# First up stage: the spread steps dealt 1, 2, 1, 2, 2 to the tiles, and a tile's first operands built ahead of the multiplication of kept results

## Chip, cores and metric

The kernel runs on 1 core of one Trainium2 chip. The metric is the device time of one execution in microseconds, median over several runs; lower is better.

## What is computed

A model of two blocks in float32, 256 tokens of width 2048 (with 16 meta tokens ahead in the first block): an HGRN2 layer, a forgetting attention layer, a layer of convolution and sliding-window attention, and at the end the PEER layer, the only part that matters here:

```python
def peer(xn, peer_w_q, peer_sub_keys, peer_u, peer_v):
    ...
    qh = (xt @ peer_w_q).reshape(T, PEER_HEADS, 2, PEER_HALF)
    sub = jnp.einsum("thpc,hpnc->thpn", qh, peer_sub_keys).astype(jnp.float32)
    ...
    experts = e1 * N_KEYS + e2
    gates = jax.nn.softmax(vals, axis=-1).astype(xn.dtype)
    def chunk_fn(args):
        xc, ec, gc = args
        u_sel = jnp.take(peer_u, ec, axis=0)
        h = jnp.einsum("cd,chkd->chk", xc, u_sel)
        a = jax.nn.gelu(h, approximate=False) * gc
        v_sel = jnp.take(peer_v, ec, axis=0)
        return jnp.einsum("chk,chkd->cd", a, v_sel)
```

Each token chooses 8 x 16 = 128 of 16,384 experts (128 x 128 keys).

## The kernel before

The kernel doesn't gather experts. It computes the product of all tokens with all experts and multiplies it by a dense table of coefficients, zero where an expert was not chosen. The experts are 128 **tiles** of 128, taken in two segments of 64. In each segment an **up stage** multiplies the tokens with tiles of `peer_u`, and a **down stage** multiplies the coefficients with tiles of `peer_v`.

Weights are float32, and each tile is split in two parts so that the product keeps its precision. For each half of a tile (1024 columns) ACT writes the high part `whi` (`split_hi`, L429), and then the low part `wlo = raw - whi` is formed (`split_lo`, L436), in this stage on DVE (`both_lo`). TensorE (PE) multiplies in `up_project` (L2060 to L2062, 48 matmuls of 256 columns a tile). DVE takes the result out of PSUM with a row factor (`hidden`, L2196), ACT applies the Gelu (L2109), and DVE multiplies that by the coefficient later (`gated`, L2201).

The table of coefficients is built by 32 **spread steps** for a segment, 8 tokens each (`STEP = 8`), and these are dealt to the tiles of the up stage by `steps_of`. A step q is, in this order:

- **operands** on DVE (`operands`): one-hot keys `e_one` (L2158), one-hot rows `e_row` (L2160) and three products `e_col` (L2164), into one of two buffers, q % 2. It waits until PE has done step q-2.
- **the step** on PE (`spread_step`, L2049): 24 small matmuls into bank 3 or 4, placed behind the tile's `up_project`. It waits for the operands, and for ACT to have emptied the same bank of step q-2.
- in the first segment alone, **the multiplication of kept results** on DVE (`multiply_kept`, L2103): 32 of the segment's 64 tiles had their product computed during the routing stage and lie in `e_coef` already; they are multiplied by the new coefficients. It waits for the step on PE, and increments `multiplied`.
- **the copy** on ACT (`spread_in_of`, L2093) of the other 32 tiles' coefficients. In the first segment it waits for `multiplied`.

Each engine runs its instructions in the order in which they are written. A round j of the loops in `up_vector`, `up_scalar` and `up_tensor` belongs to tile j; the first segment's steps begin with tile 3 and end with tile 22 (`UP_FIRST = (3, 0)`). In round j DVE also makes the low parts of tile j+1, and ACT its high parts; the multiplications for the steps of tile j stand in DVE's round j+1, the copies for them at the end of ACT's round j, so ahead of the high parts of tile j+2.

Of the kernel before, what the change touches and what calls it, by code (L numbers as in the profile page):

```python
# [153 lines left out]
def need(eng, sem, value):  # L154

    if not static(value) or value > 0:
        eng.wait_ge(sem, value)
# [57 lines left out]
def build(nc, hT_in, params_in, consts_in, masks_in, pos_in, keys_in, w_in, u_in, v_in, out):  # L215
    with ExitStack() as ctx:
# [1760 lines left out]
        STEPS = SEQ // STEP  # L1977
# [26 lines left out]
        def up_ps(q):  # L2004
            return bank[U_BANKS[q % 4]][:, 0:SEQ]
# [3 lines left out]
        def steps_of(g_, j):  # L2009

            k = j - UP_FIRST[g_]
            upto = lambda k: min((8 * k + 4) // 5, STEPS)
            return range(upto(k), upto(k + 1)) if k >= 0 else ()

        def up_plan(g_):

            last = max(j for j in range(STATIC_UP) if steps_of(g_, j))
            end = STATIC_UP if N_UP[g_] == STATIC_UP else STATIC_UP - 1
            plan, hid, act, gated = [], 0, 0, 0
            for j in range(end + 1):  # L2020
                gates = range(gated, min(gated + 5, act) if last < j < end else act if j == end else gated)
                gated = gates.stop
                hids, acts = [], []
                while act < hid and (act < N_ACT or act - N_ACT < gated):
                    acts.append(act)
                    act += 1
                while j >= UP_FIRST[g_] and hid < j and (hid < N_ACT + 2 or hid - N_ACT - 2 < gated) and hid - 2 < act:
                    hids.append(hid)
                    hid += 1
                    while act < hid and (act < N_ACT or act - N_ACT < gated):  # L2030
                        acts.append(act)
                        act += 1
                rest = range(gated, j if j == end else gated)
                gated = rest.stop
                plan.append((gates, hids, acts, rest))
            assert hid == act == gated == end
            return plan
# [59 lines left out]
        def multiply_kept(ve, q):  # L2097

            ve.wait_ge(spread, q + 1)
            if q == 0:  # L2100
                ve.wait_ge(kept, EARLY)
            now = e.coef[:, 0:EARLY, q * STEP:(q + 1) * STEP]
            ve.tensor_tensor(now, S_BANKS[q % 2][:].rearrange("p (c e) -> p e c", c=STEP)[:, 0:EARLY, :], now,  # L2103
                             ALU.mult).then_inc(multiplied, 1)
# [10 lines left out]
        def first_lo(ve, g_):  # L2115
            ve.wait_ge(coef_hi_done, g_ * SEG + 1)
            ve.tensor_tensor(e.coef_lo[:, 0, :], e.coef[:, 0, :], e.coef_first[:].bitcast(F32), ALU.subtract)\
                .then_inc(coef_split, 1)
# [34 lines left out]
        def operands(ve, g_, q):  # L2153

            b, at = q % 2, q + g_ * STEPS
            now = slice(q * STEP, (q + 1) * STEP)
            need(ve, spread, at - 1)
            ve.tensor_tensor(pairs(e.one[:, b, :, :]), keys(g_ * SEG, SEG), per_token(e.slots[:, 1, now, :], SEG),  # L2158
                             ALU.is_equal).then_inc(one_set, 1)
            ve.tensor_tensor(pairs(e.row[:, b, :, :]), keys(0, SUBKEYS), per_token(e.slots[:, 0, now, :], SUBKEYS),  # L2160
                             ALU.is_equal)
            ve.wait_ge(one_set, at + 1)
            for w in range(3):
                last = ve.tensor_tensor(pairs(e.col[:, b, w, :, :]), pairs(e.one[:, b, :, :]),  # L2164
                                        per_token(e.gates[:, w, now, :], SEG), ALU.mult)
            last.then_inc(cols_set, 1)

        def pairs(ap):
            return ap.rearrange("p t (n b) -> p t n b", b=2)

        def keys(at, n):
            return e.iota[:, at:at + n].rearrange("p (t n b) -> p t n b", t=1, b=2).broadcast_to([P, STEP, n // 2, 2])

        def per_token(ap, n):
            return ap.rearrange("p t (n b) -> p t n b", n=1).broadcast_to([P, STEP, n // 2, 2])

        def gate_parts(ve, ch):
            ve.wait_ge(slots_in, 1)
            def twice(ap):
                return ap.rearrange("p (a b) -> p a b", b=1).broadcast_to([P, SEQ, 2])  # L2180

            ch.link(ve.tensor_copy(e.gates[:, 0, :, :], twice(e.slot_gate)))
            ch.link(ve.tensor_tensor(e.rest[:, 0, :], e.slot_gate, e.gates[:, 0, :, 0], ALU.subtract))
            ch.link(ve.tensor_copy(e.gates[:, 1, :, :], twice(e.rest[:, 0, :])))
            ch.link(ve.tensor_tensor(e.rest[:, 1, :], e.rest[:, 0, :], e.gates[:, 1, :, 0], ALU.subtract))
            ch.link(ve.tensor_copy(e.gates[:, 2, :, :], twice(e.rest[:, 1, :])))

        def both_lo(ve, t):
            for half in range(2):
                split_lo(ve, t, half)  # L2190
# [7 lines left out]
        def gated(ve, g_, j):  # L2198
            ve.wait_ge(gelu_done, j + 1 + UP_BEFORE[g_])
            k = UP_AT[g_] + j  # L2200
            ve.tensor_tensor(at3(e.coef, k), one3(e.act[:, j % N_ACT, :]), at3(e.coef, k), ALU.mult)\  # L2201
                .then_inc(coef_done, 1)

        def up_vector(ve, ch, g_):
            if g_ == 0:
                gate_parts(ve, ch)
                ve.wait_ge(w_lo_done[1], T_U[0] + UP_FIRST[0] + 1 - NATIVE)
            else:
                for q in steps_of(g_, 0):
                    operands(ve, g_, q)  # L2210
                flush(ve, g_ - 1)
            last = max(j for j in range(STATIC_UP) if steps_of(g_, j))
            for j, (gates, hids, _, rest) in enumerate(up_plan(g_)):
                steps = steps_of(g_, j)
                if g_ == 0:
                    for q in steps_of(g_, j - 1):
                        multiply_kept(ve, q)
                if j or g_ == 0:
                    for q in steps[:1]:
                        operands(ve, g_, q)  # L2220
                if j < STATIC_UP and (g_ or j >= UP_FIRST[0]):
                    both_lo(ve, Tile(T_U[g_], j // 4, j % 4).next())
                if j == last + 1:
                    ve.wait_ge(spread_in, STEPS * (g_ + 1))
                for k in gates:
                    gated(ve, g_, k)
                if j == N_UP[g_]:
                    first_lo(ve, g_)
                for k in hids:
                    hidden(ve, g_, k)  # L2230
                if j or g_ == 0:
                    for q in steps[1:]:
                        operands(ve, g_, q)
                for k in rest:
                    gated(ve, g_, k)
            if N_UP[g_] == STATIC_UP:
                return

            def body(i):
                for s in range(4):  # L2240
                    j, t = 4 * i + s, Tile(T_U[g_], i, s)
                    ve.wait_ge(halves_done, 2 * t.n)
                    need(ve, gelu_done, j - 2 + UP_BEFORE[g_])
                    ve.tensor_tensor(e.hid[:, (s + 1) % 2, :], up_ps(t.q + 3), rinv[:, 0:SEQ],
                                     ALU.mult).then_inc(evacuated, 1)
                    if within(j, N_UP[g_]):
                        both_lo(ve, t.next())
                    ve.wait_ge(gelu_done, j + UP_BEFORE[g_])
                    k = UP_AT[g_] + j - 1
                    ve.tensor_tensor(at3(e.coef, k), one3(e.act[:, 2 + (s + 1) % 2, :]), at3(e.coef, k),  # L2250
                                     ALU.mult).then_inc(coef_done, 1)
                    if static(j) and j == N_UP[g_]:
                        break
            with ve.Fori(STATIC_UP // 4, N_UP[g_] // 4) as i:
                body(i)
            first_lo(ve, g_)
            body(N_UP[g_] // 4)
# [77 lines left out]
        def flush(ve, g_):  # L2335
            ve.wait_ge(halves_done, 2 * (T_V[g_] + SEG))
            for b in FLUSHED_AT:
                h2 = hT[:, 2 * b:2 * b + 2, cols_q]
                need(ve, flushed, 8 * g_)
                ve.tensor_tensor(h2, bank[b][:].rearrange("p (a b) -> p a b", a=2), h2, ALU.add).then_inc(flushed, 1)  # L2340
# [205 lines left out]
```

## Time and profile before

| | us |
|---|---|
| median of 3 runs | 3059.23 (3058.94 to 3059.59) |
| the profiled execution, its own time | 3061.99 |
| its span, first to last instruction | 3060.2 |
| PE busy | 3002.7 (98%) |
| DVE busy | 1951.2 (64%) |
| ACT busy | 1637.0 (53%) |
| mean granted clock of TensorE | 0.994 |

The first up stage's spread steps lie between 1757.8 and 1903.2 us of the span. Busy shares tell how long an engine executes; with matmuls overlapping, PE counts as busy from the start of one to the modelled end of the last. An idle time is given in square brackets ahead of the instruction that waited, with what released it. Instructions on DVE and ACT are pipelined too: one's record may end some 0.08 us after the next one's start.

### The profile page before, as it was taken

What the parts mean: (1) busy time and instruction counts of PE and PEld (TensorE: products, weight loads), DVE (VectorE), ACT (ScalarE), POOL (GpSimd) and SP (SyncE); (2) the same over time, 40 slices, a digit from 0 to 9 for tenths busy, and PEclk for the clock granted to TensorE, in tenths of its full rate; (3) what the DMA queues carried; (4) which work ended last, traced back from release to release, by engine and by line L of the source; (5) the groups of instructions that cost most, each with busy time, mean ns of one, the idle gap of its engine ahead of it and who ended that gap; (6) DMA issues with size and microseconds to landing.
All of it is one profiled execution on the core that took longest, in us unless ns stands there. A gap on an engine that the chain in (4) does not pass through costs nothing.

```text
span 3060.2 us, 63442 instructions
## 1 busy us (share of the span) xinstructions
PE 3002.7 (98%) x25220; PEld 2945.3 (96%) x25220; DVE 1951.2 (64%) x3277; ACT 1637.0 (53%) x2636; POOL 662.6 (22%) x293
## 2 busy tenths in 40 slices
PE   8999998999999999989999999999999999999999
PEld 8999998999999998769999999999999999999999
DVE  6777776744544568757777788655458865554454
ACT  5777775566788643565444434444444444444443
POOL 3333333444444432114444300000000000000000
PEclk9999999999999999989999999999999999999999
DMA  5444443554434454325555534555554455555554
GB/s 197 148 149 150 151 151 124 171 174 166 166 138 149 147 177 152 118 77 190 178 181 178 180 137 150 182 191 184 187 192 162 157 180 187 183 192 184 187 191 165
DMA packets 72288, 506.67 MB, mean 166 GB/s; under 512 B 7904, under 2 KB 10464, under 8 KB 11232
## 3 DMA queue, kind: packets, MB, share of 16 engines
q1 hardware_dynamic: 71584, 503.16, 48.3%
q8 instruction: 91, 1.49, 0.2%
q10 hardware_dynamic: 576, 1.72, 0.2%
q14 instruction: 37, 0.30, 0.0%
HBM read 502.75 MB, written 2.10 MB: 165 GB/s over the span
## 4 chain that ended last, share of the span: by engine, by line
PE 93%; DVE 5%; ACT 2%; issue 1%; DMA 0%; SPq 0%; DVEq 0%; ACTq 0%
PE bank L453 12%; PE bank L452 12%; PE bank L454 12%; PE bank L466 5%; PE bank L2284 4%; PE banks L2284 4%; PE bank L2285 4%; PE banks L2285 4%; PE bank L2286 4%; PE banks L2286 4%; PE banks L2060 3%; PE banks L2061 3%; PE banks L2062 3%; PE bank L2060 3%; PE bank L2061 3%; PE bank L2062 2%
## 5 line engine op out<-in xcount | busy, mean ns | idle before, releaser
L429 ACT ACTIVATE whi<-raw 128x1024 fp32r<-128x1024 f32 x898 | 939.2, 1057 | 946.1 <-PE bank L454 367.9
L436 DVE TENSOR_TENSOR wlo<-raw,whi 128x1024 fp32r<-128x1024 f32 x667 | 851.3, 1288 | 445.9 <-ACT whi L429 445.0
L436 POOL TENSOR_TENSOR wlo<-raw,whi 128x1024 fp32r<-128x1024 f32 x231 | 605.6, 2622 | 947.7 <-ACT whi L429 947.6
L452 PE MATMUL bank<-xa_hi,whi 128*128 128x272 f32 (+1 forms) x2000 | 581.5, 291 | 6.8 <-DVE wlo L436 5.5
L453 PE MATMUL bank<-xa_lo,whi 128*128 128x272 f32 (+1 forms) x2000 | 572.8, 286 | 0.0
L454 PE MATMUL bank<-xa_hi,wlo 128*128 128x272 f32 (+1 forms) x2000 | 571.8, 286 | 0.0
L452 PEld LDWEIGHTS bank<-xa_hi,whi 128*128 128x128 f32 x2000 | 376.6, 188 | 10.4 <-issue 7.1
L453 PEld LDWEIGHTS bank<-xa_lo,whi 128*128 128x128 f32 x2000 | 377.9, 189 | 1.3
L454 PEld LDWEIGHTS bank<-xa_hi,wlo 128*128 128x128 f32 x2000 | 376.6, 188 | 0.0
L452 PE MATMUL bank<-xb_hi,whi 128*128 128x256 f32 (+1 forms) x1120 | 317.9, 284 | 1.5 <-DVE wlo L436 1.5
L453 PE MATMUL bank<-xb_lo,whi 128*128 128x256 f32 (+1 forms) x1120 | 316.3, 282 | 0.0
L454 PE MATMUL bank<-xb_hi,wlo 128*128 128x256 f32 (+1 forms) x1120 | 315.5, 282 | 0.0
L2285 PE MATMUL bank<-e_coef_lo,whi 128*128 128x256 f32 x1024 | 286.0, 279 | 0.0
L2285 PE MATMUL banks<-e_coef_lo,whi 128*128 128x256 f32 x1024 | 285.9, 279 | 0.0
L2284 PE MATMUL bank<-e_coef_hi,whi 128*128 128x256 f32 x1008 | 282.6, 280 | 0.0
L2284 PE MATMUL banks<-e_coef_hi,whi 128*128 128x256 f32 x1008 | 282.6, 280 | 0.0
L2286 PE MATMUL bank<-e_coef_hi,wlo 128*128 128x256 f32 x1008 | 278.8, 277 | 0.0
L2286 PE MATMUL banks<-e_coef_hi,wlo 128*128 128x256 f32 x1008 | 278.7, 277 | 0.0
L2060 PE MATMUL banks<-xb_hi,whi 128*128 128x256 f32 x768 | 216.2, 282 | 1.9 <-DVE hT L2340 1.3
L2061 PE MATMUL banks<-xb_lo,whi 128*128 128x256 f32 x768 | 215.9, 281 | 0.0
L2062 PE MATMUL banks<-xb_hi,wlo 128*128 128x256 f32 x768 | 215.4, 280 | 0.0
L2061 PE MATMUL bank<-xb_lo,whi 128*128 128x256 f32 x768 | 215.4, 280 | 0.0
(453 smaller groups left out, 6779.3 us busy)
## 6 DMA issues: line engine op xcount, KB each, us to landing
raw<-in_w SPq DMA_DIRECT2D x251, 1024.0 KB, 4.8
raw<-in_v SPq DMA_DIRECT2D x128, 1024.0 KB, 5.2
raw<-in_u SPq DMA_DIRECT2D x96, 1024.0 KB, 4.9
hT<-in_hT SPq DMA_DIRECT2D x4, 544.0 KB, 8.3
out<-hT SPq DMA_DIRECT2D x8, 256.0 KB, 2.4
r_keys<-in_keys ACTq DMA_DIRECT2D x1, 1024.0 KB, 5.2
c_mask<-in_masks ACTq DMA_DIRECT2D x1, 320.0 KB, 2.9
g_mask<-in_masks SPq DMA_DIRECT2D x1, 272.0 KB, 12.3
```

Source lines behind the costliest of these rows:

```text
L429: act.activation(whi[:, (2 * t.q + half) % 4, :], raw[:, t.q, half * 1024:(half + 1) * 1024], ACT.Copy).then_inc(w_hi_done, 1)
L436: eng.tensor_tensor(wlo[:, t.q, at], raw[:, t.q, at], whi[:, slot, :].bitcast(F32), ALU.subtract).then_inc(w_lo_done[half], 1)
L452: te.matmul(ps, hi, x[0][:, kk, cols], start=(kk == 0), stop=False)
L453: te.matmul(ps, hi, x[1][:, kk, cols], start=False, stop=False)
L454: last = te.matmul(ps, lo, x[0][:, kk, cols], start=False, stop=(kk == KT - 1))
L466: last = te.matmul(ps, raw[:, t.q, kk * P:(kk + 1) * P], x[:, kk, 0:n], start=(kk == 0), stop=(kk == KT - 1))
L2060: te.matmul(ps, hi, xb[0][:, kk, 0:SEQ], start=(kk == 0), stop=False)
L2061: te.matmul(ps, hi, xb[1][:, kk, 0:SEQ], start=False, stop=False)
L2062: last = te.matmul(ps, lo, xb[0][:, kk, 0:SEQ], start=False, stop=(kk == KT - 1))
L2284: te.matmul(ps, hi, coef_hi, start=(begins and kk % 2 == 0), stop=False)
L2285: te.matmul(ps, hi, e.coef_lo[:, s % 2, :], start=False, stop=False)
L2286: last = te.matmul(ps, lo, coef_hi, start=False, stop=(final and kk % 2 == 1))
```

## The change

For the first segment `steps_of` deals the 32 steps over the same 20 tiles in another rhythm. Before, tiles 3, 4, 5, ... get 2, 2, 1, 2, 1 steps and so on in fives; now 1, 2, 1, 2, 2. The second segment keeps its rhythm. And in `up_vector` the operands of a round's first step now stand ahead of the multiplications that belong to the tile before. This touches the first segment alone, since the second has no kept results.

```diff
@@ -2009,7 +2009,7 @@
         def steps_of(g_, j):
 
             k = j - UP_FIRST[g_]
-            upto = lambda k: min((8 * k + 4) // 5, STEPS)
+            upto = lambda k: min((8 * k + (0, 4)[g_]) // 5, STEPS)
             return range(upto(k), upto(k + 1)) if k >= 0 else ()
 
@@ -2212,12 +2212,12 @@
             for j, (gates, hids, _, rest) in enumerate(up_plan(g_)):
                 steps = steps_of(g_, j)
+                if j or g_ == 0:
+                    for q in steps[:1]:
+                        operands(ve, g_, q)
                 if g_ == 0:
                     for q in steps_of(g_, j - 1):
                         multiply_kept(ve, q)
-                if j or g_ == 0:
-                    for q in steps[:1]:
-                        operands(ve, g_, q)
                 if j < STATIC_UP and (g_ or j >= UP_FIRST[0]):
                     both_lo(ve, Tile(T_U[g_], j // 4, j % 4).next())
```

What this does to DVE's queue, first in a round of the repeating part that follows on a tile with two steps (L2158 to L2164 are one step's operands, L2103 a multiplication, L436 the low parts of the next tile, L2196 the `hidden` of the tile before). Before:

```order
L2103 TENSOR_TENSOR e_coef<-bank,e_coef 128x32x8 [waits spread]
L2103 TENSOR_TENSOR e_coef<-banks,e_coef 128x32x8 [waits spread]
L2158 TENSOR_TENSOR e_one<-e_iota,e_slots 128x512 [waits spread]
L2160 TENSOR_TENSOR e_row<-e_iota,e_slots 128x1024
L2164 TENSOR_TENSOR e_col<-e_one,e_gates 128x512 [waits one_set]
L2164 TENSOR_TENSOR e_col<-e_one,e_gates 128x512 x2
L436 TENSOR_TENSOR wlo<-raw,whi 128x1024 [waits w_hi_done] x2
L2196 TENSOR_TENSOR e_hid<-banks,rinv 128x256 [waits gelu_done,halves_done]
```

And of the change:

```order
L2158 TENSOR_TENSOR e_one<-e_iota,e_slots 128x512 [waits spread]
L2160 TENSOR_TENSOR e_row<-e_iota,e_slots 128x1024
L2164 TENSOR_TENSOR e_col<-e_one,e_gates 128x512 [waits one_set]
L2164 TENSOR_TENSOR e_col<-e_one,e_gates 128x512 x2
L2103 TENSOR_TENSOR e_coef<-bank,e_coef 128x32x8 [waits spread]
L2103 TENSOR_TENSOR e_coef<-banks,e_coef 128x32x8 [waits spread]
L436 TENSOR_TENSOR wlo<-raw,whi 128x1024 [waits w_hi_done] x2
L2196 TENSOR_TENSOR e_hid<-banks,rinv 128x256 [waits gelu_done,halves_done]
```

The operands have moved from behind the multiplications to their front, so that the low parts now follow directly on a multiplication.

ACT's queue, from the copy of the first step on (L2093 a copy, L429 a half of the high parts, L2109 a Gelu). Before:

```order
L2093 ACTIVATE e_coef<-bank 128x32x8 [waits multiplied]
L2093 ACTIVATE e_coef<-banks 128x32x8 [waits multiplied]
L429 ACTIVATE whi<-raw 128x1024 [waits halves_done,w_loaded0]
L429 ACTIVATE whi<-raw 128x1024 [waits halves_done]
L2109 ACTIVATE e_act<-e_hid 128x256 [waits evacuated]
```

And of the change:

```order
L2093 ACTIVATE e_coef<-bank 128x32x8 [waits multiplied]
L429 ACTIVATE whi<-raw 128x1024 [waits halves_done,w_loaded0]
L429 ACTIVATE whi<-raw 128x1024 [waits halves_done]
L2109 ACTIVATE e_act<-e_hid 128x256 [waits evacuated]
L2093 ACTIVATE e_coef<-banks 128x32x8 [waits multiplied]
L2093 ACTIVATE e_coef<-bank 128x32x8 [waits multiplied]
```

The second step's copy has gone from the first tile to the next, where it stands with the third's; a copy still stands ahead of each pair of high parts.

## Rows read from the trace of the kernel before

**Rows 1.** Windows: us, busy PE, PEld, DVE, ACT, POOL, then PEclk, DMA share, GB/s
```profile
1780.00:1900.00 120.00, 114.86 (x1418) 112.90 (x1417) 104.80 (x209) 48.13 (x74) 0.00 (x0) 1.00 0.45 150
```

**Rows 2.** Waits, 1755.6 to 1903.1 us: total us, times, longest us
```profile
DVE e_coef L2103 <- PE banks L2049: 9.7, 11, 1.5
DVE e_coef L2103 <- PE bank L2049: 9.2, 9, 1.5
...
PE banks L2049 <- DVE e_col L2164: 7.9, 7, 4.6
...
PE bank L2049 <- DVE e_col L2164: 2.1, 5, 0.6
```

**Rows 3.** Timeline, spread steps on PE: start us, length us, operation, [idle us <- releaser]
```profile
1757.77 0.87 PE L2049 MATMUL bank<-e_col,e_row 128*128 128x64 bf16 x24 [0.23 <-DVE e_col L2164]
...
1763.29 1.46 PE L2049 MATMUL banks<-e_col,e_row 128*128 128x64 bf16 x24 [4.65 <-DVE e_col L2164]
...
1771.48 0.87 PE L2049 MATMUL bank<-e_col,e_row 128*128 128x64 bf16 x24
...
1772.19 0.86 PE L2049 MATMUL banks<-e_col,e_row 128*128 128x64 bf16 x24
...
1851.74 0.87 PE L2049 MATMUL bank<-e_col,e_row 128*128 128x64 bf16 x24
...
1858.20 0.87 PE L2049 MATMUL banks<-e_col,e_row 128*128 128x64 bf16 x24
...
1859.62 0.87 PE L2049 MATMUL bank<-e_col,e_row 128*128 128x64 bf16 x24 [0.54 <-DVE e_col L2164]
...
1902.28 0.87 PE L2049 MATMUL banks<-e_col,e_row 128*128 128x64 bf16 x24
```

**Rows 4.** Timeline, DVE at the stage's start, and behind its last operands
```profile
1755.67 0.43 DVE L2158 TENSOR_TENSOR e_one<-e_iota,e_slots 128x512 bf16<-128x512 bf16 x1
...
1760.87 0.42 DVE L2196 TENSOR_TENSOR e_hid<-bank,rinv 128x256 f32<-128x256 f32 x1 [0.22 <-ACT e_act L2109]
...
1899.02 2.35 DVE L436 TENSOR_TENSOR wlo<-raw,whi 128x1024 fp32r<-128x1024 f32 x2
```

**Rows 5.** Timeline, DVE between two spread steps of the repeating part
```profile
1852.65 0.42 DVE L2103 TENSOR_TENSOR e_coef<-bank,e_coef 128x256 f32<-128x256 f32 x1 [1.47 <-PE bank L2049]
1852.99 0.42 DVE L2158 TENSOR_TENSOR e_one<-e_iota,e_slots 128x512 bf16<-128x512 bf16 x1
...
1854.93 2.35 DVE L436 TENSOR_TENSOR wlo<-raw,whi 128x1024 fp32r<-128x1024 f32 x2
1857.21 0.42 DVE L2196 TENSOR_TENSOR e_hid<-banks,rinv 128x256 f32<-128x256 f32 x1
1857.54 0.41 DVE L2158 TENSOR_TENSOR e_one<-e_iota,e_slots 128x512 bf16<-128x512 bf16 x1
```

**Rows 6.** Timeline, DVE and ACT behind the last multiplication of kept results
```profile
1903.19 0.43 DVE L2103 TENSOR_TENSOR e_coef<-banks,e_coef 128x256 f32<-128x256 f32 x1 [1.82 <-PE banks L2049]
1905.02 2.36 DVE L436 TENSOR_TENSOR wlo<-raw,whi 128x1024 fp32r<-128x1024 f32 x2 [1.40 <-ACT whi L429]
...
1903.65 0.38 ACT L2093 ACTIVATE e_coef<-banks 128x256 f32<-128x256 f32 x1 [4.18 <-DVE e_coef L2103]
1903.93 2.00 ACT L429 ACTIVATE whi<-raw 128x1024 fp32r<-128x1024 f32 x2
```

**Rows 7.** Windows around three waits of PE (columns as in Rows 1)
```profile
1461.00:1464.00 3.00, 1.98 (x17) 1.92 (x17) 3.00 (x2) 1.57 (x2) 3.00 (x1) 1.00 0.57 164
1374.00:1378.00 4.00, 4.00 (x24) 4.00 (x23) 4.00 (x4) 2.94 (x7) 3.70 (x2) 0.59 0.98 387
1760.00:1763.00 3.00, 0.00 (x0) 0.00 (x0) 2.78 (x8) 1.17 (x3) 0.00 (x0) 0.57 0.62 262
```

**Rows 8.** Timeline, PE at two of those waits
```profile
1462.11 0.35 PE L452 MATMUL bank<-xb_hi,whi 128*128 128x256 f32 x1 [1.02 <-DVE wlo L436]
...
1373.60 0.35 PE L452 MATMUL bank<-xa_hi,whi 128*128 128x256 f32 x1 [1.85 <-DVE wlo L436]
```

## Prediction

> **What bounds the kernel now.** The page comes first: PE is busy for nearly all of the span, so a change that adds no work can only act where PE waits. The windows by stretch show the stage that the change touches: of 120 us PE is busy 114.86 and DVE 104.80 [rows 1]. The waits say for what: over the stage PE waits 7.9 + 2.1 us for `e_col`, a step's operands, the longest time 4.6 us [rows 2]. The timeline of the spread steps shows two sorts of it. The second step of the first tile starts 4.65 us late, at 1763.29 [rows 3], and later second steps wait some 0.55 us, as the one at 1859.62 does: of the twelve waits and 10.0 us [rows 2] the first step's 0.23 and the 4.65 leave ten and 5.1 us, nine of 0.55 and a last one of 0.2. A wait costs more than its idle time, since the steps' matmuls overlap: 1858.20 to 1859.62 is 1.42 us, where two steps that don't wait are 0.71 apart (1771.48 to 1772.19), so 0.71 is lost each time. A tile with one step takes 6.46 us (1851.74 to 1858.20), of which 0.71 is the step and 5.74 the tile.
>
> Why PE waits is read from DVE's timeline over one such piece [rows 5], by starts, which is how the sums below count. From PE's step at 1851.74 it is 0.91 to the multiplication (1852.65), 0.34 to the first operands (1852.99), 1.94 to the low parts (1854.93), 2.28 to `hidden` (1857.21), 0.33 to the second operands (1857.54), and 2.08 until PE starts on them (1859.62): 7.88 in all, and PE needs 6.46 + 0.71 = 7.17. So in a tile with two steps PE and DVE form a ring: multiplication, both operands, low parts and `hidden` follow one after another behind PE's last step.
>
> **The change, part by part.** No instruction is added, so all of it is order.
>
> (a) *Operands ahead of the multiplication.* DVE no longer stands still until PE's step is done: it builds operands meanwhile. Those stand-stills are 9.7 + 9.2 us in 20 waits [rows 2], or 20.5 us by starts (0.08 each more, as one record ends 0.08 after the next may start). Most of it goes.
>
> (b) *What the moved operands used to cover.* A multiplication releases ACT's copy, behind which stand ACT's high parts, for which DVE's low parts wait. The trace has this chain bare once, at the stage's end, where no operands follow a multiplication [rows 6]: multiplication 1903.19, copy 1903.65, high parts 1903.93, low parts 1905.02 after 1.40 us idle. That is 1.83 from multiplication to low parts, 0.34 of it the multiplication, so DVE stands 1.49 us by starts behind it. Before, the 1.94 us of operands between [rows 5] hid all of it, with 0.45 us to spare (1852.65 to 1854.93 is 2.28, against 1.83). Now nothing stands between. High parts are released by the last multiplication of the round, so it is paid once in each round with multiplications, 19 times (tiles 4 to 22) before the last step: 19 x 1.49 = 28.3 us. This is the term that decides.
>
> (c) *The new rhythm.* Tile 3 gets one step, so PE goes on to tile 4 at once and the second step's operands are in time. But tile 4 gets two. DVE comes to the second operands there only behind other work: from 1755.67 [rows 4] two steps' operands (3.88), two pairs of low parts (4.55), four `hidden` (1.34), one multiplication (0.34) and one stand-still (1.49), 0.3 us of waiting for a Gelu [rows 4], to 1767.5, with 2.08 for the operands 1769.6. PE could have come to it at 1757.77 + 0.71 + 0.4 (the first half of tile 4's low parts, which ends at 1755.67 + 1.94 + 1.2 = 1758.8, comes that much late) + 5.74 + 0.71 = 1765.3. So the long wait moves from tile 3 to tile 4 and is 4.3 us rather than 4.8 by starts. At the old one the granted clock fell to half (0.57 in the window [rows 7]) and the way to the next step took 8.19 us (1763.29 to 1771.48) rather than 6.46; I take these 1.73 us to come again one tile later.
>
> (d) *The sum.* With (b), is DVE or PE the bound? For five tiles with eight steps DVE needs 8 x (1.94 + 0.34) + 5 x (1.49 + 2.28 + 0.34) = 38.8 us; PE 5 x 5.74 + 8 x 0.71 = 34.4; before they took 3 x (7.17 + 0.71) + 2 x 6.46 = 36.6. So DVE binds from tile 4 on, and its work can be added up from 1755.67 to the start of the last step: operands 32 x 1.94 = 62.1; multiplications of steps 0 to 29, 30 x 0.34 = 10.2; low parts of tiles 4 to 23, 20 x 2.275 = 45.5; 20 `hidden` x 0.335 = 6.7; stand-stills 28.3; the Gelu's 0.3; and 0.7 for which the multiplication of step 3 waits for PE while its clock is low (step 3 starts at 1769.6 + 8.2 = 1777.8 and ends 0.91 later, DVE is there at 1778.1). That is 153.8, so 1909.5, and 0.1 us to PE: the last step starts at 1909.5 to 1909.6. Before it was 1902.28 [rows 3]. The same prices give the old queue up to its last operands as 62.1 + 10.5 + 43.2 + 6.7 + 20.5 + 0.3 = 143.3, or 1899.0, and the trace has the next start at 1899.02 [rows 4]. What follows on the last step is the same in both kernels. **The change costs 7.3 us**: the profiled execution (3061.99, span 3060.2) would be 3069.3 with a span of 3067.5, the median 3059.23 becomes 3066.5.
>
> A rule of the Trainium skill speaks otherwise. Here PE is busy 96% and DVE 87% of the stretch [rows 1], with 13% of DVE still free. "Perfetto Trace Analysis", section "Identifying the Most-Contended Engine", has the engine of highest occupancy as the one to work on; by that rule DVE has room, the new order costs nothing, and the time would be the first rival's below. The row on the chain behind a multiplication decides against it for me: DVE's stand-stills are no free time if another engine's answer ends them.
>
> **The rivals.**
>
> *The gap is hidden, and it is faster.* If ACT had its high parts ready in time, DVE would need 31.3 us for five tiles and PE would bind at 34.4. PE's losses at second steps go (9 x 0.71 + 0.37 = 6.7), the long wait shrinks from 4.8 to 2.8 (without the stand-still of (b)), 0.4 is new: 1902.28 - 6.7 - 2.0 + 0.4 = 1894.0, so -8.3 and 3050.9. It decides by the stand-still: five tiles take 36.6 as before at (36.6 - 18.2 - 13.1) / 5 = 1.05 us, and below that it is faster. For it speak PE's waits for operands [rows 2], against it ACT's queue, where each copy stands ahead of the high parts and waits for the multiplication, and 1.83 us measured [rows 6]. The page named above, section "Optimization Strategy", advises to let what a gap waits for start sooner; that is this rival, and the rows bear it out for the operands alone.
>
> *The clock falls too.* PE's wait at a second step now grows from 0.55 to some 1.3 us idle, some 11 times. A wait of 1.02 left the clock at 1.00, one of 1.85 stands ahead of a window at 0.59 [rows 7, 8]. If it fell each time, a waiting tile would cost 1.73 more on PE: for five tiles 3 x (7.17 + 1.73) + 2 x 6.46 = 39.6, about 40.1 with what is left of the waits, against 38.8. Over the 18 tiles from tile 5 on, 3.6 such groups, that is +4.7: +12.0 and 3071.2. TensorE's page in the Trainium skill ("TensorE: Matmul & The Clock Gate", section "HAM oscillation") describes a loop in which a wait in each tile sends the clock down in every tile; no window of this trace with waits as short as 0.55 shows it.
>
> *No measurable difference.* This needs 1.2 us or more off the sum, that is 0.06 us in each stand-still or the long wait's clock (0.7) and a little more. With a stand-still of 1.2 rather than 1.49 us it would be +1.8, so 3061.0. That the change does nothing can't be: both queues differ.
>
> **How the numbers follow.** A measurement of this kernel can tell about 0.2% (6.1 us) from no change. My sum of +7.3 is near that edge, but its prices reproduce the old queue to 0.1 us. Chances: the forecast 0.62 (3065.4 and up), the clock rival 0.12, in between 0.17, the faster rival 0.09. So slower 0.74, same 0.17, faster 0.09. The range reaches down to stand-stills shorter by 0.2 us each (19 x 0.2 = 3.8, 3062.7) and up to the clock rival with little room: 3062.5 to 3072.
>
> **What the profile of the changed kernel would show.** Right: low parts (L436) on DVE idle some 1.40 us for `whi` 19 or 20 times in the stage, from nothing before but at its end; DVE's waits before L2103 nearly gone; PE waiting for `e_col` about 12 times, once 4.1 and else 1.2 to 1.4 us; the repeating five tiles at 38.8 us; the last step near 1909.5; the second up stage as before. Wrong: L436 waits of under 1.05 us, or PE's clock under 1.00 between 1780 and 1900, or a difference that arises outside the stage.

## Result and profile after

| | us |
|---|---|
| before, median of 11 runs | 3059.86 (3058.94 to 3061.65) |
| changed, median of 11 runs | 3067.23 (3065.21 to 3068.56) |
| ratio | 1.0023, 95% interval 1.0016 to 1.0031 |
| span of the changed kernel's profiled execution | 3065.4 |

The change costs 7.4 us by the medians, where 7.3 were forecast, and the time lies in the range. It is slower, since the interval excludes 1, and just beyond the 0.2% (6.1 us) that the prediction took as its bound.

The waits of the changed kernel from 1755.6 to 1912 us, in the columns of [rows 2]:

```profile
DVE wlo L436 <- ACT whi L429: 28.0, 20, 1.4
...
PE banks L2049 <- DVE e_col L2164: 9.5, 8, 1.3
...
PE bank L2049 <- DVE e_col L2164: 5.0, 5, 1.2
...
PE banks L2060 <- DVE e_hid L2196: 1.7, 1, 1.7
DVE e_coef L2103 <- PE banks L2049: 0.6, 1, 0.6
```

DVE now stands 20 times for the high parts ahead of L436, 28.0 us in all and 1.4 at most: 19 times between the first and the last step, where before it never did, and once behind the last, as before [rows 6]. The 18.9 us in 20 waits for PE ahead of L2103 [rows 2] are all gone; the one of 0.6 belongs to the last multiplication, which lies outside [rows 2] and waited 1.82 us before [rows 6]. PE waits 14.5 us for operands rather than 10.0.

One round on DVE, where two multiplications follow on operands and the low parts on them:

```profile
1785.33 0.42 DVE L2103 TENSOR_TENSOR e_coef<-bank,e_coef 128x256 f32<-128x256 f32 x1
1785.66 0.42 DVE L2103 TENSOR_TENSOR e_coef<-banks,e_coef 128x256 f32<-128x256 f32 x1
1787.48 2.36 DVE L436 TENSOR_TENSOR wlo<-raw,whi 128x1024 fp32r<-128x1024 f32 x2 [1.40 <-ACT whi L429]
1789.76 0.42 DVE L2196 TENSOR_TENSOR e_hid<-bank,rinv 128x256 f32<-128x256 f32 x1
```

The idle time of 1.40 us is the one that [rows 6] had at the stage's end. From the last multiplication to the low parts it is 1.82 us.

PE's timeline, as in [rows 3]: the first step, the first matmul of tile 4, steps 1 and 2, two second steps five tiles apart, and the last step.

```profile
1756.62 0.87 PE L2049 MATMUL bank<-e_col,e_row 128*128 128x64 bf16 x24 [0.24 <-DVE e_col L2164]
...
1759.22 0.58 PE L2060 MATMUL banks<-xb_hi,whi 128*128 128x256 f32 x1 [1.73 <-DVE e_hid L2196]
...
1766.51 0.87 PE L2049 MATMUL banks<-e_col,e_row 128*128 128x64 bf16 x24
...
1768.51 0.87 PE L2049 MATMUL bank<-e_col,e_row 128*128 128x64 bf16 x24 [1.13 <-DVE e_col L2164]
...
1822.20 0.87 PE L2049 MATMUL banks<-e_col,e_row 128*128 128x64 bf16 x24 [1.21 <-DVE e_col L2164]
...
1860.87 0.87 PE L2049 MATMUL banks<-e_col,e_row 128*128 128x64 bf16 x24 [1.22 <-DVE e_col L2164]
...
1907.52 0.87 PE L2049 MATMUL banks<-e_col,e_row 128*128 128x64 bf16 x24 [0.99 <-DVE e_col L2164]
```

From the first step to the last it is 150.90 us, before 1902.28 - 1757.77 = 144.51: 6.4 us more. Five tiles take 38.67 us (1822.20 to 1860.87), forecast were 38.8, and 36.6 before. Behind the last step's start the rest of the span is 1157.9 us in both kernels. The first step itself starts 1.15 us earlier than before, though nothing ahead of it was changed; so the two spans differ by only 5.2 us. That is scatter between executions: in the ten profiles of this study the first step starts between 1753.86 and 1757.77, and each kernel's own times spread by 2 to 6 us. The experiments below are therefore also read by the distance from the first step to the last, which this scatter doesn't touch, called the **stage's length** here: 144.51 before, 150.90 changed.

Two windows of the changed kernel (columns as in [rows 1]):

```profile
1759.00:1762.00 3.00, 2.77 (x13) 2.78 (x14) 2.78 (x8) 1.16 (x3) 0.00 (x0) 0.54 0.58 243
1780.00:1900.00 120.00, 107.81 (x1359) 105.86 (x1357) 99.03 (x198) 42.62 (x67) 0.00 (x0) 1.00 0.41 135
```

In the first window, at the start of tile 4, the clock was mostly at the lower of its two levels (1.2 GHz); from 1780 to 1900 us it was at 1.00, in spite of PE's waits of 1.2 to 1.3 us. PE's busy time in the 120 us has fallen from 114.86 [rows 1] to 107.81.

### The profile page after: what moved, and what is told of

Same layout as the page of the kernel before. It is cut to its first block, busy times and chain, and to the rows that moved or that the text cites. A ratio compares the mean times of both kernels' runs of the same rounds, so it can differ in the third digit from the quotient of the medians.

```text
span 3065.4 us, 63442 instructions
## 1 busy us (share of the span) xinstructions
PE 3002.9 (98%) x25220; PEld 2945.7 (96%) x25220; DVE 1951.1 (64%) x3277; ACT 1636.4 (53%) x2636; POOL 662.6 (22%) x293
## 3 DMA queue, kind: packets, MB, share of 16 engines
q8 instruction: 91, 1.49, 0.2%
## 4 chain that ended last, share of the span: by engine, by line
PE 90%; DVE 6%; ACT 3%; issue 1%; DMA 0%; SPq 0%; DVEq 0%; ACTq 0%
PE bank L453 12%; PE bank L452 12%; PE bank L454 12%; PE bank L466 5%; PE bank L2284 4%; PE banks L2284 4%; PE bank L2285 4%; PE banks L2285 4%; PE bank L2286 4%; PE banks L2286 4%; PE banks L2060 2%; PE banks L2061 2%; PE banks L2062 2%; PE bank L2060 2%; PE bank L2061 2%; PE bank L2062 2%
## 5 line engine op out<-in xcount | busy, mean ns | idle before, releaser
L429 ACT ACTIVATE whi<-raw 128x1024 fp32r<-128x1024 f32 x898 | 939.2, 1057 | 945.7 <-PE bank L454 366.9
L436 DVE TENSOR_TENSOR wlo<-raw,whi 128x1024 fp32r<-128x1024 f32 x667 | 851.4, 1288 | 472.5 <-ACT whi L429 471.6
L436 POOL TENSOR_TENSOR wlo<-raw,whi 128x1024 fp32r<-128x1024 f32 x231 | 605.6, 2622 | 946.6 <-ACT whi L429 946.5
L452 PEld LDWEIGHTS bank<-xb_hi,whi 128*128 128x128 f32 x1120 | 211.2, 189 | 4.7 <-issue 2.5
```

Of the source, the lines that this page charges most:

```text
L429: act.activation(whi[:, (2 * t.q + half) % 4, :], raw[:, t.q, half * 1024:(half + 1) * 1024], ACT.Copy).then_inc(w_hi_done, 1)
L436: eng.tensor_tensor(wlo[:, t.q, at], raw[:, t.q, at], whi[:, slot, :].bitcast(F32), ALU.subtract).then_inc(w_lo_done[half], 1)
L452: te.matmul(ps, hi, x[0][:, kk, cols], start=(kk == 0), stop=False)
```

## Experiments

Theory A is that of the prediction: the stand-still behind a round's last multiplication, which ends through ACT's copy and high parts, costs the time. Theory B puts it to the new rhythm. All runs were timed beside runs of the kernel before on the same chip: its median was 3060.08 us over 28 runs for the first four kernels, 3059.83 over 16 for the others.

**The order alone.** The changed kernel with the old rhythm:

```diff
-            upto = lambda k: min((8 * k + (0, 4)[g_]) // 5, STEPS)
+            upto = lambda k: min((8 * k + 4) // 5, STEPS)
```

> The new order in DVE's queue with the old rhythm of steps (2, 2, 1, 2, 1). Theory A (the stand-still of 1.4 us idle behind the last multiplication of each round, which ends through ACT's copy and high parts, is what costs): the loss is all here, the last spread step some 7.6 us later than before against the stage's first step, +7 to +8.5 us in the time; DVE idles 19 or 20 times for whi ahead of L436. Theory B (the new rhythm costs: PE's wait at the second tile for hidden, 1.7 us, and the low clock there, while the order is free or a gain): no later than before, 0 to -6 us.

Measured: 3067.22 us (ratio 1.0023, interval 1.0013 to 1.0032), +7.1 us. Its steps on PE (first, second, last), and its wait for the high parts:

```profile
1756.98 0.87 PE L2049 MATMUL bank<-e_col,e_row 128*128 128x64 bf16 x24 [0.24 <-DVE e_col L2164]
...
1762.51 1.46 PE L2049 MATMUL banks<-e_col,e_row 128*128 128x64 bf16 x24 [4.65 <-DVE e_col L2164]
...
1909.05 0.87 PE L2049 MATMUL banks<-e_col,e_row 128*128 128x64 bf16 x24
```

```profile
DVE wlo L436 <- ACT whi L429: 28.0, 20, 1.5
```

The stage's length is 152.07, 7.56 us more than before, as expected (7.6). The whole loss is in the order, and theory B falls.

**The rhythm alone.** The kernel before with the changed line of `steps_of`:

```diff
-            upto = lambda k: min((8 * k + 4) // 5, STEPS)
+            upto = lambda k: min((8 * k + (0, 4)[g_]) // 5, STEPS)
```

> The new rhythm with the old order. Theory A: a small gain, the last spread step 2.7 us earlier than before against the first (the first tile's long wait goes, 4.65 us idle, PE's wait for hidden at the second tile, 1.7 us, and a low clock of 1.5 us come in its place, the second steps wait as before), -1.5 to -3 us. Theory B: the loss of the change is here, +5 to +8 us.

Measured: 3056.73 us (ratio 0.9989, interval 0.9980 to 0.9998), -3.4 us, a little more than the -1.5 to -3 expected. PE's timeline, with the wait at tile 4 and the two steps behind it, and two windows:

```profile
1753.86 0.87 PE L2049 MATMUL bank<-e_col,e_row 128*128 128x64 bf16 x24 [0.24 <-DVE e_col L2164]
...
1756.46 0.38 PE L2060 MATMUL banks<-xb_hi,whi 128*128 128x256 f32 x1 [1.73 <-DVE e_hid L2196]
...
1762.22 0.87 PE L2049 MATMUL banks<-e_col,e_row 128*128 128x64 bf16 x24
...
1764.26 0.87 PE L2049 MATMUL bank<-e_col,e_row 128*128 128x64 bf16 x24 [1.17 <-DVE e_col L2164]
...
1895.45 0.87 PE L2049 MATMUL banks<-e_col,e_row 128*128 128x64 bf16 x24 [0.21 <-DVE e_col L2164]
```

```profile
1756.00:1759.00 3.00, 2.54 (x21) 2.54 (x22) 2.78 (x9) 2.33 (x6) 0.00 (x0) 1.00 0.63 268
1759.00:1762.00 3.00, 3.00 (x28) 3.00 (x27) 3.00 (x5) 1.03 (x2) 0.00 (x0) 1.00 0.00 0
```

The stage's length is 141.59, 2.9 us less than before. Here the clock stayed at 1.00 behind the same wait of 1.73 us: tile 4 took 5.76 us (1756.46 to 1762.22), where the changed kernel's took 7.29. That the length comes so near to the 2.7 us expected is partly luck: the low clock, put at 1.5 us, didn't come, but the second step of tile 4 waited 1.17 us for its operands and lost 1.33 by starts, which the expectation didn't have.

The two parts don't add up. Apart they give 7.56 - 2.92 = 4.64 us of length, together 6.39: with the new order DVE is the bound, and the rhythm, which saves on PE, is worth only 1.2 us there (152.07 to 150.90).

**High parts ahead of the copies.** The changed kernel, and on ACT:

```diff
+                if g_ == 0:
+                    for q in steps_of(g_, j - 1):
+                        spread_in_of(act, g_, q)
                 for k in acts:
                     gelu(act, g_, k)
-                for q in steps_of(g_, j):
-                    spread_in_of(act, g_, q)
+                if g_:
+                    for q in steps_of(g_, j):
+                        spread_in_of(act, g_, q)
```

> The changed kernel, but on ACT the copies of a tile's steps stand behind the high parts of the next round and not ahead of them, so that the high parts no longer wait for the multiplication. No instruction is added or taken. Theory A: the stand-stills on DVE ahead of L436 go, PE becomes the bound, the last spread step is 8.8 us earlier than before and the low parts behind it 10.3 us: -8.5 to -10.5 us against before, PE's waits for e_col under 2 us in all. Theory B: ACT's order matters nothing, as the changed kernel, +6 to +8 us. Theory C (DVE is bound by the sum of its work and the gaps only fill time in which it would wait anyway): gaps go, waits ahead of L2103 come in their place, +3 to +7 us.

Measured: 3050.63 us (ratio 0.9968, interval 0.9956 to 0.9980), -9.5 us against before and so some 17 against the changed kernel. DVE's timeline at a last multiplication, the waits in the stage, and the first and last step (the edit moves later line numbers by 4):

```profile
1803.86 0.42 DVE L2103 TENSOR_TENSOR e_coef<-bank,e_coef 128x256 f32<-128x256 f32 x1
1804.19 2.35 DVE L436 TENSOR_TENSOR wlo<-raw,whi 128x1024 fp32r<-128x1024 f32 x2
```

```profile
DVE e_one L2162 <- PE bank L2049: 6.3, 4, 1.8
DVE e_one L2162 <- PE banks L2049: 4.9, 4, 1.5
DVE wlo L436 <- ACT whi L429: 4.3, 3, 1.4
...
PE banks L2049 <- DVE e_col L2168: 0.6, 3, 0.2
...
PE bank L2049 <- DVE e_col L2168: 0.2, 1, 0.2
```

```profile
1756.06 0.87 PE L2049 MATMUL bank<-e_col,e_row 128*128 128x64 bf16 x24 [0.25 <-DVE e_col L2168]
...
1891.64 0.87 PE L2049 MATMUL banks<-e_col,e_row 128*128 128x64 bf16 x24
```

The low parts follow on the multiplication at once (0.33 us by starts); the three waits for `whi` that are left lie behind the last step, at 1899.68 and later. The stage's length is 135.58, 8.9 us less than before. DVE waits for PE again, 11.2 us ahead of its operands, but PE waits only 0.8 us for them: PE is the bound. Theory A holds and C falls, since no wait of DVE for PE took the gap's place at PE's cost.

**Hidden in the gap.** The changed kernel, and in `up_vector`:

```diff
+                early = g_ == 0 and UP_FIRST[0] < j <= last
+                if early:
+                    for k in hids:
+                        hidden(ve, g_, k)
                 if j < STATIC_UP and (g_ or j >= UP_FIRST[0]):
                     both_lo(ve, Tile(T_U[g_], j // 4, j % 4).next())
...
-                for k in hids:
-                    hidden(ve, g_, k)
+                if not early:
+                    for k in hids:
+                        hidden(ve, g_, k)
```

> The changed kernel, but in rounds 4 to 22 hidden (0.335 us by starts, 17 of them) stands between the multiplication and the low parts, so that it lies in the stand-still. Theory A: 17 x 0.335 = 5.7 us of DVE's chain go, DVE's idle ahead of L436 is 1.07 us rather than 1.40 where hidden stands there, the time is +0.5 to +2 us against before (the changed kernel less 5.7). Theory B: as the changed kernel, +6 to +8 us.

Measured: 3061.00 us (ratio 1.0002, interval 0.9993 to 1.0011), +0.9 us. DVE's timeline, and the first and last step:

```profile
1807.46 0.42 DVE L2103 TENSOR_TENSOR e_coef<-bank,e_coef 128x256 f32<-128x256 f32 x1
1807.79 0.42 DVE L2196 TENSOR_TENSOR e_hid<-bank,rinv 128x256 f32<-128x256 f32 x1
1809.27 2.36 DVE L436 TENSOR_TENSOR wlo<-raw,whi 128x1024 fp32r<-128x1024 f32 x2 [1.06 <-ACT whi L429]
```

```profile
1756.74 0.87 PE L2049 MATMUL bank<-e_col,e_row 128*128 128x64 bf16 x24 [0.25 <-DVE e_col L2164]
...
1902.02 0.87 PE L2049 MATMUL banks<-e_col,e_row 128*128 128x64 bf16 x24 [0.99 <-DVE e_col L2164]
```

Of the 1.40 us idle 1.06 are left, and the stage's length is 145.28: 5.6 us less than in the changed kernel for 17 times 0.335 = 5.7 us put into the gap. So the loss follows the size of the gap one to one. The repeating five tiles take 37.01 us (1782.66 to 1819.67), where they took 36.6 before; 1.15 us of the gap are left by starts, so order and gap would balance with 0.09 less, at 1.06 us, where the prediction had 1.05. That last point is worked out, not run.

**Both operands in the gap.** The changed kernel, and the second step's operands moved from the round's end to behind the multiplications:

```diff
                     for q in steps_of(g_, j - 1):
                         multiply_kept(ve, q)
+                    for q in steps[1:]:
+                        operands(ve, g_, q)
...
-                if j or g_ == 0:
+                if j and g_:
                     for q in steps[1:]:
                         operands(ve, g_, q)
```

> The changed kernel, but a round's second operands stand behind the multiplication and ahead of the low parts, where DVE stands still, and not behind hidden. ACT's queue is as in the changed kernel. Theory A (the stand-still behind the last multiplication costs): it is filled in each round with two steps and stays 1.40 us idle in the rounds with one, where DVE has that much room; PE is the bound, its waits for e_col under 1 us, the last spread step 9.8 to 11.4 us earlier against the first than before (the lower figure if the clock falls at the second tile): -10 to -11.5 us in the time. If what counts were ACT's order by itself rather than DVE's stand-still, it would stay near the changed kernel, +4 to +7 us.

Measured: 3051.49 us (ratio 0.9970, interval 0.9958 to 0.9982), -8.3 us by the medians, short of the -10 to -11.5 expected, of which the interval (-12.9 to -5.5 us) takes in all; the stage's length is 134.53, 10.0 us less than before, as expected with a low clock at tile 4. The gap is filled with DVE's own work and ACT is left as it was, so ACT's order costs only through DVE's stand-still.

```profile
1757.63 0.87 PE L2049 MATMUL bank<-e_col,e_row 128*128 128x64 bf16 x24 [0.25 <-DVE e_col L2164]
...
1892.16 0.86 PE L2049 MATMUL banks<-e_col,e_row 128*128 128x64 bf16 x24
```

```profile
DVE wlo L436 <- ACT whi L429: 15.5, 11, 1.4
...
PE bank L2049 <- DVE e_col L2164: 0.2, 1, 0.2
```

Of the 11 waits for `whi` seven lie ahead of the last step, 1.40 us idle each, in rounds with one step. There they cost nothing, since PE waits only 0.2 us for operands; the other four lie behind the last step.

**The first hidden earlier.** As the last one, and in round 3 `hidden` of tile 0 ahead of the low parts, as PE's tile 4 takes the bank that it frees:

```diff
+                if g_ == 0:
+                    for k in hids:
+                        if k == 0:
+                            hidden(ve, g_, k)
                 if j < STATIC_UP and (g_ or j >= UP_FIRST[0]):
                     both_lo(ve, Tile(T_U[g_], j // 4, j % 4).next())
...
                 for k in hids:
-                    hidden(ve, g_, k)
+                    if g_ or k:
+                        hidden(ve, g_, k)
```

> As the one with both operands in the gap, and the first hidden stands ahead of the first low parts in round 3, as PE's second tile waits 1.73 us for it. If PE is the bound there: the wait falls to some 0.6 to 0.7 us idle, 1.1 us less, and the clock may stay up at the second tile (another 1.5 us): -11 to -12.5 us against before. If DVE is still the bound: no change against the one before it.

Measured: 3048.15 us (ratio 0.9963, interval 0.9949 to 0.9976), -11.7 us. First step, first matmul of tile 4, step 1, last step:

```profile
1755.44 0.87 PE L2049 MATMUL bank<-e_col,e_row 128*128 128x64 bf16 x24 [0.23 <-DVE e_col L2164]
...
1756.99 0.35 PE L2060 MATMUL banks<-xb_hi,whi 128*128 128x256 f32 x1 [0.68 <-DVE wlo L436]
...
1762.72 0.87 PE L2049 MATMUL banks<-e_col,e_row 128*128 128x64 bf16 x24
...
1887.61 0.86 PE L2049 MATMUL banks<-e_col,e_row 128*128 128x64 bf16 x24
```

PE's wait ahead of tile 4 is 0.68 rather than 1.73 us and for the low parts now. That is the wait of which the prediction thought in the changed kernel; by starts it is 0.84 us, with 0.34 of it the `hidden` put ahead, against the 0.4 of the prediction. The stage's length is 132.17.

**The high parts first as well.** As the last one, with the ACT edit above.

> As the one with the first hidden earlier, and the high parts ahead of the copies on ACT. If DVE's queue has no stand-still left that matters, only the stage's end gains: the low parts behind the last multiplication come 1.3 us earlier and PE's wait for hidden there (0.55 us idle) goes: -11.5 to -13 us against before.

Measured: 3046.11 us (ratio 0.9959, interval 0.9945 to 0.9972), -13.7 us against before, 0.7 more than the expected range allowed, and 21 against the changed kernel; the interval overlaps that of the kernel ahead of it, so by the times alone the two can't be told apart. First and last step, and PE's waits in the stage:

```profile
1754.55 0.87 PE L2049 MATMUL bank<-e_col,e_row 128*128 128x64 bf16 x24 [0.25 <-DVE e_col L2168]
...
1886.45 0.86 PE L2049 MATMUL banks<-e_col,e_row 128*128 128x64 bf16 x24
```

```profile
PE banks L2060 <- DVE wlo L436: 0.7, 1, 0.7
...
PE bank L2049 <- DVE e_col L2168: 0.2, 1, 0.2
```

The stage's length is 131.90, where the prediction's prices for PE alone, 19 x 5.74 + 31 x 0.71, give 131.1. The wait behind the last step, for `hidden`, is gone, and what follows on the last step is 0.8 us shorter (1157.05 rather than 1157.9). This version has the lowest median of the study, and it beats both kernels.

**The kernel before with the high parts first.** The ACT edit and nothing else.

> The kernel before, with the high parts ahead of the copies on ACT and nothing else. Theory A: the operands cover the chain there (0.45 us to spare), so the last spread step comes when it did, and only the end gains some 0.5 us: 0 to -1 us. A theory by which ACT's order costs in any case would have it some 8 to 9 us faster, as with the high parts first in the changed kernel.

Measured: 3058.84 us (ratio 0.9998, interval 0.9989 to 1.0007), -1.0 us. First and last step:

```profile
1753.94 0.87 PE L2049 MATMUL bank<-e_col,e_row 128*128 128x64 bf16 x24 [0.24 <-DVE e_col L2168]
...
1898.01 0.87 PE L2049 MATMUL banks<-e_col,e_row 128*128 128x64 bf16 x24
```

The stage's length is 144.07, 0.4 us less, and that lies where the clock was low at the stage's start: from the second step to the third it took 7.69 us (1759.46 to 1767.15) rather than 8.19. Another 0.8 us are saved behind the last step, where the chain lay bare. ACT's order is worth nothing where operands cover the chain, and 15 us of the stage's length (150.90 to 135.58) where they don't.

## Why the prediction was right

- **(a) The waits for PE go.** Right: 18.9 us in 20 waits before, none of them after.
- **(b) The stand-still that the operands used to cover.** Right in place, size and number: 1.40 us idle in each of 19 rounds. It was read from one pair of rows at the stage's end [rows 6], which showed the chain bare. The hidden-in-the-gap run shows that the loss follows it one to one, and two runs that take it away by different means (ACT's order, DVE's order) both end well below the kernel before.
- **(c) The new rhythm.** The place was right, the size not. "The long wait moves from tile 3 to tile 4 and is 4.3 us rather than 4.8 by starts" failed: PE waits 1.13 us idle for step 2, 1.29 by starts. DVE had the operands when they were forecast (11.89 us after the first step, forecast 11.9), but PE came later than the 7.6 us that were forecast. It waited 1.73 us idle at the head of tile 4 for `hidden` of tile 0, whose bank it needs and which stands behind the low parts on DVE, where I had put 0.4 us for the low parts; and the low clock came in tile 4, 1.55 us, rather than in tile 5, 1.73. The long wait before had hidden that bank's wait. While DVE is the bound this changes nothing but one term: with the clock up in tile 5, DVE's multiplication of step 3 doesn't wait 0.7 us.
- **(d) The sum.** Step 31 forecast 7.3 us later, the stage's length grew by 6.4; 0.7 of the rest is that term; 0.2 is left, which the rounding of the prices could make and which was not traced. The sum of the old queue, 143.3, was a weaker test than it sounds, since it took its 20.5 us of stand-stills from the trace itself. The medians' 7.4 is nearer to the forecast than its working deserves: in part that is luck, as scatter between executions is of the size of the difference.
- **The rivals.** The gap was not hidden in the changed kernel. The first rival's 3050.9 is what the run with the high parts first gives (3050.63), with that rival's mechanism: the gap is hidden and PE binds. The parts of its sum differ, though: no long wait of 2.8 us came, the wait for `hidden` (1.73 idle) did, and 0.8 us of the gain lies behind the last step; so that the two times agree is partly luck. The clock rival fell: 1.00 from 1780 to 1900 us with PE's waits of 1.2 to 1.3 us. The loop of which the Trainium skill tells in "TensorE: Matmul & The Clock Gate", section "HAM oscillation", didn't arise with waits of this size in any run here. The Trainium skill's rule in "Perfetto Trace Analysis", section "Identifying the Most-Contended Engine", would have had DVE's free 13% carry the new order; the trace disagrees: from 1780 to 1900 us of the changed kernel PE is busy 90% and DVE 83%, and yet DVE's queue sets the pace, as what counted was whose answer ended its idle time. With that idle time gone, in the run with the high parts first, PE binds as the rule has it.

## What to carry over

Before an instruction is moved ahead of one that another engine waits for, ask what the moved one was covering behind it: here 1.94 us of operands covered an answer that takes 1.49 us, and moving them saved waits for PE and paid the answer in each of 19 rounds. A chain that is hidden nearly everywhere is often bare at one end of a loop, and its price can be read there. The cure was to fill the gap with work that isn't needed for the answer (the second operands), or to put what the other engine owes ahead of what it waits for.

## What was not expected of the hardware

The same wait of PE did not have the same effect on its clock. At the head of tile 4, with 1.73 us idle behind the same instructions, the window from 1759 to 1762 us had the clock at 0.54 in the changed kernel, and both windows from 1756 to 1762 us had it at 1.00 in the run with the rhythm alone, whose first step lay 2.76 us earlier; tile 4 took 7.29 and 5.76 us. Of the five profiles with this wait the other three, those with the high parts first, with `hidden` in the gap and with both operands in the gap, had the tile at 7.28 or 7.29 us. With that wait at 0.68 us both profiles had the tile at full speed: with the first `hidden` earlier 5.73 us (1756.99 to 1762.72), and with the high parts first as well 5.72 (1756.11 to 1761.83). Behind the wait of 4.65 us at tile 3, too, the way to the next step differed between kernels with the same work on PE there: 8.19 us before, 8.27 with the order alone and 7.69 with only the high parts first. So whether a wait of 1.73 us halves the clock can't be told from its length alone. That this makes part of the scatter between executions of one kernel is likely but not shown: of the 16 runs of the kernel before in the second group, those with a mean clock of 0.993 took 3060.82 to 3062.96 us and those with 0.996 took 3057.19 to 3059.85, but only one execution of each kernel was profiled.
